# One core, two transformer blocks: even first steps of the differential attention, and the second scan of the gated recurrence begun inside the first

## The reference

```python
# differential attention, 8 heads, two maps each
sc = einsum('bqhcd,bkhcd->bhcqk', qblk, k) * scale
p = softmax(sc)
w = p[:, :, 0] - lambda_full * p[:, :, 1]
o = einsum('bhqk,bkhe->bqhe', w, v)
o = rms(o, subln, 1e-5) * (1.0 - lambda_init)

# gated recurrence, 8 heads of 128, forward and backward, summed
q = silu(q_raw); f = lb + (1 - lb) * sigmoid(f_raw); k = (1 - lb) * sigmoid(-f_raw)
state_t = state_{t-1} * f_t + k_t (outer) v_t;   o_t = q_t . state_t
y = group_rmsnorm(o_forward + o_backward, norm_g) * silu(g_out)
```

## Time and profile before

| | us |
|---|---|
| median of 3 runs | 2515.18 |
| lowest, highest | 2513.99, 2522.87 |
| profiled execution | 2519.92 |
| its span | 2518.1 |
| TensorE busy | 2456.8 (98%) |
| VectorE busy | 1790.1 (71%) |
| ScalarE busy | 1449.0 (58%) |
| GpSimd busy | 258.8 (10%) |

### The profile page before, as it was taken

One profiled execution on the slowest core, in us unless ns is written; L12 is line 12 of the kernel. 1 busy time (PEld: TensorE's weight loads), 2 busy tenths in 40 slices (PEclk: granted clock), 3 DMA queues, 4 the chain that ended last, 5 costly groups with the idle time before them and its releaser, 6 DMA issues.

```text
span 2518.1 us, 42226 instructions
## 1 busy us (share of the span) xinstructions
PE 2456.8 (98%) x17296; PEld 2255.5 (90%) x17296; DVE 1790.1 (71%) x2897; ACT 1449.0 (58%) x2122; POOL 258.8 (10%) x222
## 2 busy tenths in 40 slices
PE   8999999999999999899999999999999999999998
PEld 8888999888889898799999799998898999899997
DVE  5567675565576755587868887885597778887875
ACT  5547555445465554477565655664766656556654
POOL 0000002000000000000113720000010106500000
PEclk9999999999999999899999999999999999999999
DMA  7543476655434566554466645555554467645663
GB/s 258 152 135 119 159 249 194 203 180 157 130 117 151 184 194 202 161 151 128 125 198 191 196 136 190 186 183 194 154 152 125 138 196 204 184 151 183 192 207 127
DMA packets 358916, 430.44 MB, mean 171 GB/s; under 512 B 20616, under 2 KB 286310, under 8 KB 358468
## 3 DMA queue, kind: packets, MB, share of 16 engines
q1 hardware_dynamic: 341312, 401.72, 51.1%
q10 hardware_dynamic: 14340, 14.93, 2.6%
q0 software_dynamic: 3072, 11.10, 1.4%
HBM read 424.44 MB, written 3.24 MB: 170 GB/s over the span
## 4 chain that ended last, share of the span: by engine, by line
PE 88%; DVE 7%; ACT 3%; issue 1%; DMA 1%; POOL 0%; POOLq 0%; ACTq 0%; DVEq 0%
PE ps L112 85%; PE ps L115 2%; DVE wlo L121 1%; ACT L118 1%; ACT hgKm L118 1%; ACT whi L118 0%; ACT E L118 0%; ACT lnv L118 0%; DVE hgQB L121 0%; DMA kT<-in_diff_lambda 0%; DVE hgQF L121 0%; DVE E L124 0%; DVE sbc L130 0%; DVE E L133 0%; DVE hgKm L121 0%
## 5 line engine op out<-in xcount | busy, mean ns | idle before, releaser
L121 DVE TENSOR_TENSOR wlo<-wring,whi 128x1024 fp32r<-128x1024 f32 (+1 forms) x768 | 920.2, 1218 | 257.0 <-ACT whi L118 256.2
L118 ACT ACTIVATE whi<-wring 128x1024 fp32r<-128x1024 f32 (+1 forms) x768 | 802.8, 1054 | 431.3 <-PE ps L112 405.2
L112 PE MATMUL ps<-uT,whi 128*128 128x256 f32 x4640 | 822.2, 281 | 6.7 <-DVE wlo L121 5.0
L112 PEld LDWEIGHTS ps<-uT,whi 128*128 128x128 f32 x4640 | 706.7, 188 | 16.1 <-DVE wlo L121 8.2
L112 PE MATMUL ps<-uT,wlo 128*128 128x256 f32 x2320 | 646.8, 279 | 0.0
L112 PEld LDWEIGHTS ps<-uT,wlo 128*128 128x128 f32 x2320 | 438.9, 189 | 0.0
L112 PE MATMUL ps<-xT,whi 128*128 128x256 f32 x2112 | 378.1, 283 | 2.5 <-DVE xT L121 1.3
L112 PEld LDWEIGHTS ps<-xT,whi 128*128 128x128 f32 x2112 | 321.8, 188 | 10.2 <-issue 6.2
L112 PE MATMUL ps<-xT,wlo 128*128 128x256 f32 x1056 | 294.6, 279 | 0.0
L112 PE MATMUL ps<-whi,hid 128*128 128x512 f32 x864 | 270.4, 392 | 1.6 <-DVE wlo L121 1.6
L112 PEld LDWEIGHTS ps<-xT,wlo 128*128 128x128 f32 x1056 | 198.2, 188 | 0.3
(11 more groups left out here) (395 smaller groups left out, 3570.6 us busy)
## 6 DMA issues: line engine op xcount, KB each, us to landing
wring<-in_w_in SPq DMA_DIRECT2D x346, 512.0 KB, 4.2
wring<-in_mlp_w SPq DMA_DIRECT2D x128, 512.0 KB, 4.3
wring<-in_w_up SPq DMA_DIRECT2D x88, 512.0 KB, 4.5
wring<-in_w_down SPq DMA_DIRECT2D x44, 512.0 KB, 4.4
wring<-in_w_branch SPq DMA_DIRECT2D x32, 512.0 KB, 3.3
wring<-in_w_out SPq DMA_DIRECT2D x32, 512.0 KB, 4.5
wring<-in_mem_w_kv SPq DMA_DIRECT2D x16, 512.0 KB, 6.3
wring<-in_w_br_hg SPq DMA_DIRECT2D x16, 512.0 KB, 5.2
```

The lines of the kernel that those rows point to most:

```text
L112: return self.e.matmul(*p, **k) if self.e else Nothing()
L118: return self.e.activation(*p, **k) if self.e else Nothing()
L121: return self.e.tensor_tensor(*p, **k) if self.e else Nothing()
```

## The change

Differential attention: `staged` gets `even=True`; a stage with a yield of its own then yields also while it has no head yet. One more `yield` stands before it.

Gated recurrence: (1) in `hg_proj` the output gate is projected before the values, and the last `forget_scale` follows its first panel; (2) `hg_scan(0)` is given the second scan as `following` and advances it by three steps between its own last ones (start and split; first products, first merge and first copy; first scaling and products); (3) `by_panels` lets a projection pass one panel per turn and the weights are 1.22 to 1 and 1.1 to 1; (4) the level -1 copy is a new step `hg_first` on ScalarE, directly behind the first merge; (5) `hg_start` waits for the first scan's last level products, `hg_split` for its cross products, and the squares of the first scan lie over `B0.kf`; (6) `hg_scale` signals each of its four scalings, and merges and cross products wait for just the one that they read.

```diff
-def staged(n, *stages):
+def staged(n, *stages, even=False):
     for i in range(n + max(lag for _, lag, _ in stages)):
         for f, lag, rest in stages:
             if 0 <= i - lag < n:
                 f(i - lag)
                 if rest or i >= n:
                     yield
+            elif even and rest and i < lag:
+                yield
...
+    def by_panels(g):
+        n = len(panels)
+        for _ in g:
+            if len(panels) > n:
+                n = len(panels)
+                yield
...
+            yield
             yield from staged(8, (scores(0), 0, True), (scores(1), 0, True), (lambda h: turn_unit(un[h, 0]), 1, True), (values, 2, True),
-                              (norm, 3, False), (weights, 0, False), (gain, 4, False))
+                              (norm, 3, False), (weights, 0, False), (gain, 4, False), even=True)
...
+            B.g = ar.take("hgg", 1024, at=o + 6144)
+            to_g = projB(w, GG + c0, 512, uT, features_to(B.g, ACT.Silu))
+            next(to_g)
+            do("forget_scale", *pend.pop())
+            yield
+            yield from to_g
             B.v = ar.take("hgv", 1024, at=o + 5120)
             yield from projA(w, GI + c0, 512, uT, tokens_to(B.v, 512))
-            do("forget_scale", *pend.pop())
-            B.g = ar.take("hgg", 1024, at=o + 6144)
-            yield from projB(w, GG + c0, 512, uT, features_to(B.g, ACT.Silu))
-        def hg_scan(hf, B, W):
+        def hg_scan(hf, B, W, following=None):
...
             do("hg_merge", B, 0)
+            do("hg_first", B, us)
             yield
-            do("hg_level", B, -1, us)
...
             yield
-            yield
+            if not hf:
+                some(following, 1)
+                yield
...
-        weave((hg_scan(0, B0, W), 1), (hg_proj(1, B1), 1.3))
+        second = hg_scan(1, B1, W)
+        weave((hg_scan(0, B0, W, second), 1.22), (by_panels(hg_proj(1, B1)), 1))
...
-        weave((hg_scan(1, B1, W), 1), (two_gates(), 1))
+        weave((second, 1.1), (by_panels(two_gates()), 1))
...
     def hg_merge(B, j):     # ScalarE; QB on GpSimd likewise
-            e.wait_ge(*at(("hgscaled", B.tag, j - 1)))
+            e.wait_ge(*at(("hgscaled", B.tag, j - 1, "QF")))
...
+    def hg_first(B, us):    # ScalarE
+        if B.last:
+            e.wait_ge(*at(("yhraw", B.last, 2)))
+        for st in range(2):
+            e.wait_ge(*at(us[st].full))
+            e.activation(B.W.A4[:, st, :, st * 128:st * 128 + 128], us[st].ap.rearrange("p (h t) -> p h t", h=4), ACT.Copy)
...
     def hg_start(B):        # VectorE
         if B.last:
-            e.wait_ge(*at(("yh", B.c.l, B.hf * 4 - 1)))
+            e.wait_ge(*at(("hgprod", B.last, 6)))
...
     def hg_split(B):
+        if B.last:
+            e.wait_ge(*at(("hgcross", B.last)))
```

More of the change, by code:

```diff
@@ L1032, in hg_scan @@
             yield
-            yield
+            if not hf:
+                some(following, 1)
+                yield
             def values(h):
-                B.sq[h] = W.sq.take()
+                B.sq[h] = W.sq[hf].take()
                 do("hg_values", B, c, h, AB.take(), yh)
@@ L1059, in hg_work @@
             W.QK = [[ar.take("hgQm", 1024, at=13824 + 2048 * i), ar.take("hgKm", 1024, at=14848 + 2048 * i)] for i in range(2)]
-            W.sq = Slots([Buf("hgsq", 0, 512, W.QK[0][1].ap[:, o:o + 512]) for o in (0, 512)])
+            W.sq = [Slots([Buf("hgsq", 0, 512, b.ap[:, o:o + 512]) for o in (0, 512)]) for b in (B0.kf, W.QK[0][1])]
             W.A4 = W.At.ap.rearrange("p (s h t) -> p s h t", s=2, h=4)
@@ L1559, in hg_cross @@
     def hg_cross(B, us):
-        e.wait_ge(*at(("hgscaled", B.tag, 6)))
+        e.wait_ge(*at(("hgscaled", B.tag, 6, "kb")))
         for st, k, q in ((0, B.kf, B.W.QF), (1, B.kb, B.W.QB)):
@@ L1567, in hg_cross @@
                 m = e.matmul(p3[:, h, :], k4[:, h, st * 128:st * 128 + 128], q4[:, h, 128 - st * 128:256 - st * 128], start=True, stop=True)
-            m.then_inc(*up("pe_level", u.full))
+            m.then_inc(*up("pe_level", u.full, *([("hgcross", B.tag)] if st else [])))
     def hg_values(B, c, h, u, yh):
@@ L1911, in hg_merge @@
         e.activation(halves(Qm, 1, n), halves(B.W.QF, 1, n), ACT.Copy).then_inc(*up("act_hg", ("hgQF", B.tag, j)))
+        if j >= 1:
+            e.wait_ge(*at(("hgscaled", B.tag, j - 1, "kf")))
         e.activation(halves(Km, 0, n), halves(B.kf, 0, n), ACT.Copy)
+        if j >= 1:
+            e.wait_ge(*at(("hgscaled", B.tag, j - 1, "kb")))
         e.activation(halves(Km, 1, n), halves(B.kb, 1, n), ACT.Copy).then_inc(*up("act_hg", ("hgK", B.tag, j)))
+    def hg_first(B, us):
[3 more added lines that the diff above has]
+            e.wait_ge(*at(us[st].full))
+            e.activation(B.W.A4[:, st, :, st * 128:st * 128 + 128], us[st].ap.rearrange("p (h t) -> p h t", h=4), ACT.Copy).then_inc(
+                *up("act_hg", us[st].key, ("hglevel", B.tag, st, -1)))
     def hg_cross(B, us):
@@ L2041, in scalar_program @@
                  merged=merged, ln_stats=ln_stats, ln_out=ln_out, relu_square=relu_square, square_part=square_part, square_rows=square_rows, rms_scale=rms_scale, small_gates=small_gates,
-                 cumsum_rows=cumsum_rows, store_rows=store_rows, store_max=store_max, spread_rows=spread_rows, ml_max_cols=ml_max_cols, forget_out=forget_out, hg_merge=hg_merge, hg_cross=hg_cross,
+                 cumsum_rows=cumsum_rows, store_rows=store_rows, store_max=store_max, spread_rows=spread_rows, ml_max_cols=ml_max_cols, forget_out=forget_out, hg_merge=hg_merge, hg_first=hg_first, hg_cross=hg_cross,
                  hg_values=hg_values, hg_norm=hg_norm, ssd_conv=ssd_conv, ssd_silu=ssd_silu, ssd_turn=ssd_turn,
@@ L2475, in hg_level @@
             p3 = u.ap.rearrange("p (h t) -> p h t", h=4)
[L2476 to L2480, removed]
             mask = cst[:, C_M + 128 * j:C_M + 128 * j + 128].bitcast(U32).rearrange("p (h t) -> p h t", h=1).to_broadcast([128, 4, 128])
@@ L2499, in hg_scale @@
         e.wait_ge(*now("dve_hg"))
-        for x, side, T, ev in ((W.QF, 1, Tf, "hgQF"), (B.kf, 0, Tf, "hgK"), (W.QB, 0, Tb, "hgQB"), (B.kb, 1, Tb, "hgK")):
+        for x, side, T, ev, name in ((W.QF, 1, Tf, "hgQF", "QF"), (B.kf, 0, Tf, "hgK", "kf"), (W.QB, 0, Tb, "hgQB", "QB"), (B.kb, 1, Tb, "hgK", "kb")):
             e.wait_ge(*at((ev, B.tag, j)))
-            o = e.tensor_tensor(half(x, side), half(x, side), tb(T, 1 - side), ALU.mult)
+            e.tensor_tensor(half(x, side), half(x, side), tb(T, 1 - side), ALU.mult).then_inc(*up("dve_hg", ("hgscaled", B.tag, j, name)))
         if j < 6:
             e.tensor_tensor(W.Tf[j % 2].ap[:, 0:nb], tp(Tf, 0), tp(Tf, 1), ALU.mult)
-            o = e.tensor_tensor(W.Tb[j % 2].ap[:, 0:nb], tp(Tb, 0), tp(Tb, 1), ALU.mult)
-        o.then_inc(*up("dve_hg", ("hgscaled", B.tag, j)))
+            e.tensor_tensor(W.Tb[j % 2].ap[:, 0:nb], tp(Tb, 0), tp(Tb, 1), ALU.mult).then_inc(*up("dve_hg"))
     def hg_rows(B, c, h, yh):
@@ L2761, in hg_merge @@
             e.wait_ge(*at(("hgprod", B.tag, j - 2)))
-            e.wait_ge(*at(("hgscaled", B.tag, j - 1)))
+            e.wait_ge(*at(("hgscaled", B.tag, j - 1, "QB")))
         else:
```

## The result

| | before | after |
|---|---|---|
| median of 5 runs, us | 2516.99 | 2498.89 |
| lowest, highest | 2513.99, 2522.87 | 2489.89, 2502.31 |
| profiled execution | 2519.92 | 2502.31 |
| its span | 2518.1 | 2500.5 |
| mean granted clock | 0.992 | 0.995 |

The ratio is 0.9919, 95% interval 0.9893 to 0.9945: faster by 0.8%. The forecast was 2498.5. (The two more executions of the kernel before moved its median from the 2515.18 that I started from to 2516.99, so the gain between the medians is 18.1 us, where I had forecast 16.7.)

A forecast was written before the change was run, and what follows sets the result against it. TensorE, busy for 98% of the span, was taken as the bound, so only waits, halved clock or pace could change the time. Recurrence 13.8 plus attention 2.9 gave 16.7 us: 2515.2 - 16.7 = 2498.5, range 2488 to 2509 (8 in 10).

The forecast's parts named there:

- Recurrence, 13.8 forecast: Gated recurrence, both layers: 7.4 us of waits and halved clock removed per layer, less 0.5 charged; 13.8 us.
- The 0.5 I charged for ScalarE's tail: First scan's tail: ScalarE's merges queue behind norms, new waits of 0.5 us per layer, bounds 0 and 3.9.
- The walk along ScalarE's list: From TensorE's norm 0: ScalarE 10.9 us against TensorE 9.7 with 0.8 head start, then 9.9 against 10.2; about level.
- the first scan's 1.25 us: First scan: losses of 0.85 and 0.40 us per layer go through the copy on ScalarE and finer signals.
- Attention, 2.9 forecast: Differential attention, both layers: 1.3 us gained per layer, 1.7 of halved clock, 0.7 lost per layer; 2.9 us.
- the wait at turn 1: Attention's second turn: 2.07 us wait for VectorE's weights shrinks; VectorE done at 16.2, TensorE there at 15.9.
- the 0.7 us per layer charged to the memory branch's first turn: End of attention: last norm directly before the branch's scores, turn ready after 8.5 us, TensorE at 7.8; bounds 0 and 3.
- Rival 1: First scan's tail: wait moves to ScalarE, 3 us plus 1.7 of halved clock per layer; 2507 us; chance 0.13.
- Rival 2: Up-projection stages: one flips its matmul pace, 9.5 us; 2508 if slow, 2489 if fast; chance 0.12, half each way.
- Rival 3: Whole kernel: the removed clock drops, 5.1 us, come back elsewhere; 2503.6 us; chance 0.09.
- the rule that I weighed against the sum: Clock: gated by recent busyness, drop's place varies by run; three removed drops (5.1 us) may return on remaining waits.
- Rival 4: Recurrence tail: three early steps each wait for a norm, 11.7 us, plus 3.4 of clock per layer; 2528; chance 0.04.

The follow-up runs named there:

- x7: Changed kernel with the second scan's first-level copy done three times over on ScalarE (four more copies, 2.6 us): 2498.27 us in one execution.
- x4: Kernel before plus only the recurrence's local edits (copy on ScalarE, finer signals, looser waits, gate before values), old scan order and weights: 2514.94 us, ratio 0.9983.
- x5: Changed kernel without the attention's edits, first-level copy on VectorE, one signal behind all four scalings; new scan order and weights: 2508.14 us, ratio 0.9959 to before.
- x8: Changed kernel with twelve more first-level copies of the second scan on ScalarE, 7.8 us: 2516.31 us in one execution.
- x12: Changed kernel without `even=True`, its extra yield kept, and two more yields before the last turn of weights: 2490.37 us, ratio 0.9888 to the kernel before.

## Why the prediction was right

**Median and mechanism held.** 2498.5 forecast, 2498.89 measured; for the profiled execution 2503.2 forecast, 2502.31 measured. That the number was hit this closely is luck. Two misses of opposite sign are in it: the attention gave 2.7 us more than forecast, and pace and clock elsewhere took about 2 us; and the executions of the changed kernel alone lie 12 us apart.

**Recurrence, 13.8 forecast, 13.9 measured.** The waits per layer (0.85 + 0.40 + 1.75 + 2.73 = 5.73) measured 6.0 and 5.9 in the rest; the clock's 1.7 measured 1.7 in both. The 0.5 I charged for ScalarE's tail is not there, and the pace excess took 1.0 and 0.5 in its place, so that the sum fits by accident to the tenth. The walk along ScalarE's list came out right as a walk: level. Merge 1 had 0.35 us to spare, and `x7` shows that 2.6 us more on the list already cost 1.5 us.

**One gain was put down to a part that was not needed.** I gave the first scan's 1.25 us to the copy and the finer signals. They remove most of it (`x4`), but `x5` has neither and no loss at all. No panel more stands in TensorE's list there: the kernel before and `x5` have the same projection matmuls between the eight products of the levels (24, 48, 24, 48, 48, 24, 48). What differs is VectorE's list. In `x5` the copy stands ahead of a panel split instead of behind it, and the weights put another split ahead of the first masked merge. In the kernel before, one split of this stretch takes 1.68 us instead of 1.22, and another waits 0.49 us for ScalarE's high part; in `x5` none does either. That other split, before and in `x5`:

```profile
1128.46 1.23 DVE L121 TENSOR_TENSOR wlo<-wring,whi 128x1024 fp32r<-128x1024 f32 x1 [0.49 <-ACT whi L118]
```

```profile
1129.73 1.22 DVE L121 TENSOR_TENSOR wlo<-wring,whi 128x1024 fp32r<-128x1024 f32 x1
```

Counted from the stage's start, the next scaling begins at 59.11 us before and at 58.38 in `x5`. The 0.49 us is what VectorE lacked to 20 in the earlier trace rows (19.51); after the change it is busy for 20.00 of 20 us, so its load was not what had to shrink. Which of the two shifts does it, the copy's place or the weights', I have not separated; I had counted both at nothing.

**Attention, 2.9 forecast, 5.6 measured.** The first step that failed is the wait at turn 1: of its 2.07 us 0.3 were to stay, and 0.05 did. The wait at turn 0, forecast at 0.5, measured 0.57 from start to start:

```profile
183.48 0.85 PE L115 MATMUL ps<-cst,E 128*128 128x128 f32 x4 [0.50 <-DVE E L130]
```

Two more steps failed. First, said that E was waited for four times, 5.4 us, and I had spoken for the second turn of each layer, 4.14; the other two are the last turn's, in the kernel before

```profile
234.32 0.85 PE L115 MATMUL ps<-cst,E 128*128 128x128 f32 x4 [0.61 <-DVE E L130]
```

and they went as well, 0.61 and 0.70 us of idle time. Second, the 0.7 us per layer charged to the memory branch's first turn was not there. After the change the norm, the branch's scores and the turn stand as

```profile
252.86 1.02 PE L112 MATMUL ps<-dsq,cst 128*128 128x512 f32 x2
253.72 1.03 PE L112 MATMUL ps<-mk,mqT 128*128 128x256 f32 x4
...
257.41 1.03 PE L112 MATMUL ps<-mk,mqT 128*128 128x256 f32 x4
...
261.12 0.72 PE L115 MATMUL ps<-cst,E 128*128 128x128 f32 x4
```

with no wait on any: the norm moved to its place before the scores, as forecast, but the turn came 8.26 us after it, not 7.8, and VectorE was in time. The half clock after the wait in layer 2 (1.7) went, as forecast. Together: 2.2 and 2.3 us less of waits in the two layers, 0.3 us lost again in each to the score groups, and 1.7.

**A premise that was too narrow.** I wrote that the time can change only by waits, the halved clock or the pace. The order of TensorE's own operations is a fourth way: a broken pair of score groups costs 1.14 us without any wait, and the forecast has no term for it. The change itself lost only some 0.3 us per layer by it, so the forecast stood.

**The rivals.** Rival 1 (ScalarE waits of 3 us) did not happen; in `x7`, with 2.6 us more on ScalarE, the wait is 1.2 us. Rival 2 happened to a part: the pace excess over the whole execution was 20.7 us before and 24.4 after, but 15.9 in the change repeated. Rival 3 did not happen in the profiled run but did in the repetition: the four stages have no half clock in either, yet all half-clock stretches add up to 40.1 us before, 28.6 after and 38.3 in the repetition, where two of them, from 52.9 and 1763.0 us, are new or longer. So 5.8 us were saved in the one and 0.9 in the other: what the rule that I weighed against the sum allows, drops that come back elsewhere, is seen in one of two executions. Rival 4 was real as a mechanism, and `x8` shows its price; the change has no wait of this kind, with 0.35 us to spare at merge 1.

## What to carry to other kernels

Read the row of waits to its last count: four waits of 5.4 us with only two of them explained is a row not yet read. Waits behind a full engine went away by order alone (`x5`), so before work is moved to another engine a run with another order of the same work is worth it. And when products over 64 rows come in twos, look in the trace whether they start in pairs: a weave that puts a panel between them cost 1.14 us each time here, and no view of waits shows it.

## What the runs showed of the hardware that I had not expected

**The pace changes from execution to execution.** The same kernel, two executions, the same stretches; columns as the earlier trace rows. The change, then its repetition:

```profile
870.00:890.00 20.00, 20.00 (x172) 20.00 (x171) 15.16 (x17) 11.00 (x14) 0.00 (x0) 1.00 0.61 191
1600.00:1620.00 20.00, 20.00 (x172) 20.00 (x171) 16.95 (x27) 12.28 (x17) 0.00 (x0) 1.00 0.58 179
```

```profile
870.00:890.00 20.00, 20.00 (x179) 20.00 (x179) 14.24 (x17) 12.57 (x16) 0.00 (x0) 1.00 0.65 209
1600.00:1620.00 20.00, 20.00 (x178) 20.00 (x178) 16.93 (x27) 13.51 (x20) 0.00 (x0) 1.00 0.67 210
```

In such a stage TensorE starts a matmul of 256 columns every 0.113 or every 0.118 us on average, all through, at clock 1.00 and with no wait. Over 14 executions (one of each kernel, two of the change) the excess was between 15.7 and 28.2 us. That spread, 12.5 us, is not much less than the gain of the whole change. What sets it is open. The recurrence, in contrast, had the same excess (3.3 us) in eleven of sixteen stages that ran its changed order.

**Half-clock stretches.** Those that follow a wait in the changed parts left with it. Those between the blocks and at the end stayed in every execution, and their length varied: from about 1030 us on 13.7 us at 0.50 before, 10.2 after, 13.7 in the repetition, 6.8 in `x12`.
